# A tuned one-core kernel: sinks loaded as whole rows, an earlier h_lo and later additions on VectorE, and three more low parts a stage on GpSimd

## The reference

```
u = modulate(rmsnorm(x, norm_g[l, 0]), ada[0], ada[1])
x = x + 0.5 * ada[2] * swiglu(u, w_ff1_up[l], w_ff1_down[l])      # FF, width 2816
u = modulate(rmsnorm(x, norm_g[l, 1]), ada[3], ada[4])
x = x + ada[5] * token_mixing(u, ..., sinks[l], ...)              # attention with sinks + pooling
u = modulate(rmsnorm(x, norm_g[l, 2]), ada[6], ada[7])
x = x + 0.5 * ada[8] * swiglu(u, w_ff2_up[l], w_ff2_down[l])      # FF
```

## Time and profile before

| | |
|---|---|
| median of 3 runs | 2001.8 us (2000.57 to 2002.77) |
| the profiled execution's own time | 1999.01 us |
| its span | 1997.2 us |
| mean granted TensorE clock | 0.993 of full speed |
| busy: PE, DVE, ACT, POOL | 1954.4, 1491.7, 852.6, 108.8 us |
| weights and other data moved by DMA | 265.23 MB, mean 133 GB/s |

### The profile page before, as it was taken

The page is one execution under the profiler, slowest core; times in us unless marked ns, Lnnn a source line. Parts: engine busy times, 40 slices in busy tenths (PEclk is TensorE's granted clock), DMA queues, the critical chain, the costliest instruction groups (busy, mean ns, idle before and its releaser), DMA issues.

```text
span 1997.2 us, 31967 instructions
## 1 busy us (share of the span) xinstructions
PE 1954.4 (98%) x12475; PEld 1753.9 (88%) x12475; DVE 1491.7 (75%) x2333; ACT 852.6 (43%) x1495; POOL 108.8 (5%) x81
## 2 busy tenths in 40 slices
PE   9979999999999999999999999999999999999999
PEld 7769989887788889999998999998777888999998
DVE  5878888685767778888787888977766868668672
ACT  3424536333522535354453535454343235345351
POOL 1000000301000000000300000020200000000002
PEclk9989999999999999999999999999999999999999
DMA  9654453534444344544444454444534433334332
GB/s 299 195 129 137 133 158 112 138 111 148 148 144 161 85 127 125 160 138 117 148 132 122 129 165 124 133 148 83 166 122 158 143 95 84 98 95 118 103 102 79
DMA packets 343908, 265.23 MB, mean 133 GB/s; under 512 B 49358, under 2 KB 326018, under 8 KB 343760
## 3 DMA queue, kind: packets, MB, share of 16 engines
q1 hardware_dynamic: 342960, 262.63, 44.2%
q0 software_dynamic: 496, 0.37, 0.3%
q10 hardware_dynamic: 304, 0.19, 0.0%
HBM read 261.07 MB, written 2.10 MB: 132 GB/s over the span
## 4 chain that ended last, share of the span: by engine, by line
PE 87%; DVE 5%; ACT 3%; issue 2%; DMA 2%; SPq 1%; ACTq 0%; DVEq 0%
PE bank L2373 11%; PE bank L2375 11%; PE bank L2374 11%; PE bank L2214 10%; PE bank L2215 10%; PE bank L2216 10%; PE ps L2214 4%; PE ps L2215 4%; PE ps L2216 4%; PE bank L2298 2%; PE bank L2299 1%; PE bank L2302 1%; ACT w_hi L1009 1%; DVE ada_acc L1561 1%; PE ps L2375 1%
## 5 line engine op out<-in xcount | busy, mean ns | idle before, releaser
L2373 PE MATMUL bank<-u_hi,w_hi 128*128 128x256 f32 x1120 | 317.8, 284 | 11.1 <-issue 9.5
L2374 PE MATMUL bank<-u_lo,w_hi 128*128 128x256 f32 x1120 | 317.4, 283 | 0.0
L1009 ACT ACTIVATE w_hi<-stage 128x1024 fp32r<-128x1024 f32 (+3 forms) x259 | 219.7, 867 | 174.7 <-DMA stage<-in_w_pool_o 49.3
L1402 DVE TENSOR_TENSOR w_lo<-stage,w_hi 128x1024 fp32r<-128x1024 f32 (+2 forms) x226 | 218.8, 974 | 68.2 <-ACT w_hi L1009 67.1
L2214 PE MATMUL bank<-u_hi,w_hi 128*128 128x512 f32 x648 | 258.8, 399 | 0.3 <-DVE prod L1664 0.3
L2216 PE MATMUL bank<-u_hi,w_lo 128*128 128x512 f32 x648 | 252.6, 390 | 0.0
L2215 PE MATMUL bank<-u_lo,w_hi 128*128 128x512 f32 x648 | 252.4, 390 | 0.0
L2375 PE MATMUL bank<-u_hi,w_lo 128*128 128x256 f32 x840 | 238.2, 284 | 0.0
L2373 PEld LDWEIGHTS bank<-u_hi,w_hi 128*128 128x128 f32 x1120 | 215.4, 192 | 13.7 <-issue 10.7
L2374 PEld LDWEIGHTS bank<-u_lo,w_hi 128*128 128x128 f32 x1120 | 215.4, 192 | 0.9
L1025 ACT ACTIVATE w_hi<-stage 128x512 fp32r<-128x512 f32 (+1 forms) x210 | 157.2, 768 | 118.5 <-PE bank L2375 42.0
(11 more groups left out here) (291 smaller groups left out, 4357.2 us busy)
## 6 DMA issues: line engine op xcount, KB each, us to landing
stage<-in_w_ff_up SPq DMA_DIRECT2D x172, 512.0 KB
ada_stage<-in_w_ada SPq DMA_DIRECT2D x80, 512.0 KB, 4.5
ada_stage_mix<-in_w_ada SPq DMA_DIRECT2D x48, 512.0 KB, 4.6
stage<-in_w_ff_down SPq DMA_DIRECT2D x24, 960.0 KB
stage<-in_w_in SPq DMA_DIRECT2D x16, 1024.0 KB
stage<-in_w_ff_down SPq DMA_DIRECT2D x16, 896.0 KB
ada_block<-in_w_ada SPq DMA_DIRECT2D x8, 1024.0 KB, 11.9
stage<-in_w_out SPq DMA_DIRECT2D x8, 1024.0 KB
```

Source lines behind the costliest of these rows:

```text
L1009: nc.scalar.activation(hi_tile(e, key), raw_tile(stage, e, key), ACT.Copy).then_inc(hi_ready, 1)
L1402: nc.vector.tensor_tensor(raw_tile(w_lo, e, key), raw_tile(stage, e, key), hi_tile(e, key), ALU.subtract).then_inc(lo_ready, 1)
L2373: mm(dst, hi[:, k, :], r_hi_[:, k, :], start=(k == 0 and w in (1, 7)), stop=False, skip_group_check=True)
L2374: mm(dst, hi[:, k, :], r_lo_[:, k, :], start=False, stop=False, skip_group_check=True)
```

## The change

1. `positions_load`: the sinks come in one transfer that gives each of the 128 partitions the whole table (16 numbers), in place of four transfers, each to 64 partitions, of single numbers taken two apart. `sink_all` gets a last axis of 2, and the mixer's `neg_sink` is made in two halves, each by an operation of 64 partitions. The count that VectorE waits for falls with the number of transfers.
2. `first_plain_tiles`, first stage: VectorE makes h_lo of pair 4 ahead of the pieces of w_ada at that place.
3. FF stages that another stage follows: VectorE no longer makes the low parts of the next stage's tiles 0, 1 and 2; GpSimd's `last_down` makes them behind its own eight.
4. Mixer to FF: VectorE makes the low part of the next stage's tile 1 behind `close_first`, and tile 2's is GpSimd's (`third_tile`).
5. `to_next`: the last addition of squares moves from ahead of `normalise` to behind its second scaling (`scaled(1)`).
6. `plain_tiles` waits till the low parts of the first three tiles are there.

```
         def positions_load():
...
-                with nc.allow_non_contiguous_dma(reason="eight sinks"):
-                    for i in range(DEPTH):
-                        for t in range(2):
-
-                            pool.dma_start(sink_all[t * CHUNK:(t + 1) * CHUNK, i, :],
-                                          sinks[i].rearrange("(b t) -> t b", t=2)[t].partition_broadcast(CHUNK)
-                                          ).then_inc(late_in, 16)
+                pool.dma_start(sink_all.rearrange("p l b t -> p (l b t)")[:, :],
+                               sinks.rearrange("l h -> (l h)").partition_broadcast(P)).then_inc(late_in, 16)
...
         def last_down(e):
...
                 for m in range(KT):
                     low_part(e, ("D", PARTS - 1, m))
+                for n in range(AHEAD if e + 1 < STAGES else 0):
+                    low_part(e + 1, first_tile(e + 1, n))
+
+            def third_tile(e):
+
+                pool.wait_ge(lo_ready, LO_BASE[e] + AHEAD - 1)
+                low_part(e, first_tile(e, AHEAD - 1))
...
+                third_tile(event(l, 2))
                 last_down(event(l, 2))
...
             def normalise(l, i, last_update=None):
...
                     scaled(q)
+                    if last_update and q == 1:
+                        add_squares(event(l, i), KT - 1)
...
             def to_next(l, i, done):
...
                 close_second(l, i, 0, done)
-                add_squares(event(l, i) + 1, KT - 1)
                 normalise(*divmod(event(l, i) + 1, 3), lambda: close_second(l, i, 1, done))
...
                 low_part(e, ("D", 0, 1))
+                low_h(e, 4)
                 pieces(e, ("U", 10))
-                plain_pair(e, 5)
+                plain_product(e, 5)
...
             def plain_tiles(e):
                 f = first_pair(e)
+                dve.wait_ge(lo_ready, LO_BASE[e] + AHEAD)
...
-                ahead = final and e + 1 < STAGES
                 for m in range(KT):
-                    if ahead and m == KT - 2:
-                        low_part(e + 1, first_tile(e + 1, 1))
...
-                    if ahead and m == KT - 3:
-                        dve.wait_ge(lo_ready, lo_done(e, ("D", p, KT - 1)))
-                        low_part(e + 1, first_tile(e + 1, 0))
-                    if ahead and m == KT - 2:
-                        low_part(e + 1, first_tile(e + 1, 2))
...
                 for n in range(MIX_TILES):
-                    if not T_V <= n < T_OUT:
+                    if not T_V <= n < T_OUT and n < MIX_TILES - 2:
                         low_ahead(e, n + AHEAD)
...
                     if n == 0:
-                        nc.vector.tensor_scalar(neg_sink[:, :], sink_all[:, l, :], -1.0, None, ALU.mult).then_inc(sink_ready, 1)
+                        for t in range(2):
+                            half = slice(t * CHUNK, (t + 1) * CHUNK)
+                            ins = nc.vector.tensor_scalar(neg_sink[half, :], sink_all[half, l, :, t], -1.0, None, ALU.mult)
+                        ins.then_inc(sink_ready, 1)
...
                     elif n == MIX_TILES - 2:
                         close_first(l, 1)
+                        low_ahead(e, n + AHEAD)
```

More of the change, by code:

```diff
@@ L411, in trunk @@
         lay = at("lay", [P, N_ROWS], F32, region(N_ROWS * 4))
-        sink_all = at("sink_all", [P, DEPTH, 4], F32, region(DEPTH * 16))
+        sink_all = at("sink_all", [P, DEPTH, 4, 2], F32, region(DEPTH * 32))
         c_act = at("c_act", [P, KT], F32, region(KT * 4))
@@ L751, in vec_before @@
             return l * VEC_STEPS + 2 * i - 1
-        N_LATE = 16 * (2 * DEPTH + 1)
+        N_LATE = 16 * 2
         block = ctx.enter_context(nc.Block())
```

## The result

The changed kernel took 1985.03 us in the median of 4 runs (1981.53 to 1985.65), the kernel before 2001.88 in the runs compared with it; the ratio is 0.9913 with a 95% interval of 0.9896 to 0.993. That is 17 us less, as forecast in sign and size (1985, range 1979 to 1992). The profiled executions differ by less: 1985.02 against 1999.01, spans of 1983.2 and 1997.2, 14.0 us. Part of the study is about where such executions differ.

A forecast was written before the change was run, and what follows sets the result against it. TensorE was taken as the bound, busy 98% of the span, with only 42.8 us idle and low-clock stretches to win. 12.5 + 6.0 − 1.0 − 0.4 = 17.1 us took the median 2001.8 to about 1985, range 1979 to 1992.

The forecast's parts named there:

- Then the item lands 9.8 us earlier: First stage: with sinks as whole rows costing near nothing, the load of weight item 6 lands 9.8 us earlier.
- 12.5 us: First stage, sinks and h_lo together: TensorE starts item 6 9.8 us earlier, plus 2.7 us of clock.
- still lands a few us late: Rival, first stage: item 6's load stays a few us late through neighbours on its queue; 1990 us, chance 0.10.
- Covered by the late load: First stage: early h_lo alone only brings TensorE to its dry point at 120.6 instead of 123.17.
- 2.40 us at 101.78 did not: First stage: the 2.40 us wait for h_lo lost no clock, so 1.5 us of idling is too little to.
- 3.0 us each: Mixer to FF, two places: next stage's first matmul about 665.6 against 668.65, 6.0 us for the two.
- loss 1.0: FF to FF, one place: GpSimd's low parts hold sq_sum and nw_t, nw_y 1.4 us later, 0.4 returned; loss 1.0 us.
- 0.4 for both: FF to mixer, two places: nw_t stands beside GpSimd's low part; loss 0.4 us for both, after part is given back.
- small operations aren't held: Rival, stage transitions: VectorE's small operations don't stand still beside GpSimd's low parts; 29 us gain, 1973 us, chance 0.08.
- the clock falls anyway: Rival, mixer's places and FF to FF: clock falls to 0.50 at all three, 5 us less gain, 1990 us, chance 0.16.
- Whole rows are no cheaper: Rival, first stage: 128 packets at 0.33 us cost today's 42.3 engine-us, the 12.5 go; 1997.2 us, chance 0.04.
- the slower rival: Rival, first stage: the new transfer's 128 packets at 0.62 us take 5.2 us longer; 2002.4 us, chance 0.03.

The follow-up runs named there:

- e10_latepos: e7_gate with GpSimd's positions and sinks transfers issued only after the first part's last low part: 1974.97 us, ratio 0.9863.
- e2_hlo: The kernel before with h_lo ahead of the pieces alone: 1999.84 us against 2000.93, ratio 1.0.
- e6_nohlo: The changed kernel with h_lo back behind the pieces: 1981.92 us, ratio 0.9907.
- e1_rows: The kernel before with the sinks as whole rows alone: 1990.64 us against 2000.93, ratio 0.9951.
- e3_pool: The kernel before with only the three low parts behind an FF stage's last part moved from VectorE to GpSimd: 2002.97 us against 2000.93, ratio 1.0012.
- e7_gate: The changed kernel, but GpSimd begins the third tile's low part only when nw_y is made: 1977.51 us, ratio 0.9881.
- e8_nopool: The changed kernel with the low parts behind the last part of an FF stage back on VectorE: 1982.44 us, ratio 0.9904.

## Why the prediction was right, and where it was not

- **The whole.** 1985 was forecast and 1985.03 measured. The sum of terms was 17.1 us against the profiled execution; the profiled executions differ by 14.0. I had added the profiled before's distance to its median, 2.8 us, to a sum that was 3.1 us too large for the profiles; the changed kernel's profile lies at its median, and the two errors met. Within the sum, too, 4.4 us missing in the first stage and 1.7 at the mixer's places stand against 3.0 us more than forecast at FF to mixer, where kernels with the old code gain as much. The value is in part luck; the mechanisms, one by one, are not.
- **Sinks as whole rows (the mechanism right, the size off).** "Then the item lands 9.8 us earlier" and "12.5 us" for the two startup edits: VectorE began 8.15 us earlier, and the stage ended 8.1 us ahead. I took the landing from a place where nothing of GpSimd's queue was under way, and left the positions, in rows 4's own queue just ahead of the sinks, out of it. Against e10_latepos, which moves them away and has my 12.5, the 4.3 us that the changed kernel lacks are 1.7 for the later start of item 6, 1.6 for the clock behind it, and 1.1 at the third wait, where executions differ. A load that "still lands a few us late" was among the rivals, at 0.10, put down to its neighbours on its own queue. The reason that I gave for the price, that a packet's time goes with its pieces, is not shown: a packet of 64 bytes took 1.04 us in the mean before, one of 512 bytes 0.03 after.
- **h_lo.** "Covered by the late load" was right (e2_hlo: 0). That 1.5 us of idling would be left was wrong (3.29; and 123.17 less 2.40 is 120.8, not the 120.6 that it was worked out from), and so that the clock would stay: it fell. "2.40 us at 101.78 did not" was one execution; behind the same wait it fell in four of seven. With the load as late as it was, the edit gave nothing that can be told (e6_nohlo).
- **Mixer to FF, "3.0 us each".** 1.9 and 2.4 in the profiled pair, some 4 at the first of the two against the executions of the same old code in e1_rows, e2_hlo and e3_pool. The mechanism was as told: the sum no longer waits for w_hi. TensorE's wait for it is 1.86 and 1.26 (forecast 1.2), nw_t stands (1.98), the clock stays at 1.00. What was mis-sized is that wait, 1.86 for 1.2 at the first place; what I had not seen is that the old order's fall of the clock varies, since I had one execution.
- **FF to FF, "loss 1.0".** 0.89, by the mechanism told: sq_sum 2.56, nw_t 2.10, nw_y late.
- **FF to mixer, "0.4 for both".** The table shows +1.0 and +1.6, but kernels with the old code show as much. No effect of the change can be told there; the hold of nw_t (2.13) is as forecast, and takes the place of VectorE's own low part.
- **The rival "small operations aren't held"** is refuted by five rows of nw_t of about 2 us. The Trainium skill ("SBUF — State Buffer", Who interferes with whom) says that a VectorE instruction with two SBUF inputs contends with a GpSimd one that reads SBUF, and calls the shared ports an exclusive lock. The trace agrees down to 2 columns: nw_t, begun at 386.91, ends at 389.04, and the low part beside it at 389.02. RECIPROCAL, with one input, took 0.17 us beside the same low part.
- **The rival "the clock falls anyway"** happened in the first stage, where I had priced it for the transitions: 1.6 us against e10_latepos.
- **"Whole rows are no cheaper" and the slower rival** fell: e1_rows is 9.8 us faster.

## What to carry to other kernels

In this kernel, work handed to GpSimd wasn't off VectorE's path as long as it ran beside VectorE's short operations with two SBUF inputs: start it behind them, not when its own input is ready (e7_gate: 6.4 us for two waits). A gain that sits ahead of a later wait is worth nothing until that wait goes; here h_lo was covered by a load, and the load was held in part by the positions. And size a place from several executions: one profile may have met it at its best.

## What the runs showed of the hardware that I had not expected

- **The same idle time, another clock.** Behind the same wait of 2.40 us for h_lo the clock stayed in three kernels and fell in four, as told above. Ahead of item 6 TensorE idled 2.60 us in e7_gate and 2.61 in e8_nopool, and in the 6 us from 123.5 the granted clock was 1.00 in the one and 0.72 in the other. The windows of e7_gate and of e8_nopool:

```profile
123.50:129.50 6.00, 6.00 (x37) 5.39 (x38) 5.93 (x9) 1.35 (x2) 0.00 (x0) 1.00 0.01 3
```

```profile
123.50:129.50 6.00, 6.00 (x26) 5.02 (x25) 5.90 (x10) 0.37 (x1) 0.00 (x0) 0.72 0.02 5
```

  That fall costs 1.6 us. Behind the whole first stage the two stand 10.13 and 6.46 us ahead of before; 2.4 us of this difference lie at the third wait, 1.69 in the one and 2.53 with a second fall in the other. The window of e8_nopool there:

```profile
206.00:212.00 6.00, 6.00 (x25) 4.97 (x25) 5.90 (x10) 0.60 (x2) 0.00 (x0) 0.72 0.00 0
```

  So the length of a wait doesn't decide by itself whether the clock falls to 1.2 GHz behind it; what does stays open here.
- **A few KB can hold the engines for 6 us.** Four transfers of 1 KB in 4-byte pieces held back a load of 512 KB by about 8 us (16.7 from issue to use before, 8.6 after); the one transfer of 8 KB in rows of 64 bytes takes 0.4 us of engine time. What it costs the load behind it no run shows apart from the positions.
